# A block kernel on one core: the gemm steps of a recurrence's scan stand behind two of its three small products

## What is computed

```
h = rms_norm(x, pre_norm_gain); proj = h @ w_in
# per head (8 heads of 64), for each of the 1024 rows t:
sa    = state @ a_t
state = state * decay_t + outer(sa, b_t) + outer(v_t, k_t)
y_t   = state @ r_t
# gates: sigmoid(g_attn) * y_attn + sigmoid(g_rwkv) * y_rwkv, z_rwkv in silu
```

## Time and profile before

| | us |
|---|---|
| runs, median of 3 | 2829.97 |
| runs, lowest and highest | 2827.18, 2830.27 |
| profiled execution, its own time | 2842.01 |
| its span, first to last instruction | 2840.2 |
| PE busy in it | 2707.1 (95%) |
| DVE, ACT, POOL busy | 1264.2, 810.1, 1040.2 |
| scan of pair 0, from its first L780 to its last L780 | 785.25 to 842.11 |
| scan of pair 3, likewise | 1288.87 to 1346.89 |

### The profile page before, as it was taken

How to read it: one execution, slowest core, us unless ns; L and a number is a source line. 1 busy time by engine, 2 the same in 40 slices (tenths; PEclk the granted TensorE clock), 3 DMA queues, 4 the chain that set the end, 5 groups by cost and what they waited for, 6 DMA issues and landing times.

```text
span 2840.2 us, 44277 instructions
## 1 busy us (share of the span) xinstructions
PE 2707.1 (95%) x17968; PEld 2176.6 (77%) x17968; DVE 1264.2 (45%) x2338; ACT 810.1 (29%) x1607; POOL 1040.2 (37%) x1318
## 2 busy tenths in 40 slices
PE   6999999997999999999898999999998998999999
PEld 5787777875867777686787888788887887777777
DVE  4225252435847466484531433533335003377743
ACT  3444444444113131220212211211113003255531
POOL 2223232232322231321455133344444456435442
PEclk9999999998999999999998899999999996999999
DMA  3111111111101010111331211111111121111122
GB/s 125 41 45 41 42 45 49 45 45 38 35 17 55 28 49 28 34 46 61 152 119 61 74 45 46 43 45 45 45 45 38 52 67 56 45 38 45 43 109 84
DMA packets 200907, 154.02 MB, mean 54 GB/s; under 512 B 5120, under 2 KB 183680, under 8 KB 200064
## 3 DMA queue, kind: packets, MB, share of 16 engines
q1 hardware_dynamic: 186256, 106.44, 12.6%
q10 hardware_dynamic: 14448, 44.74, 4.1%
HBM read 128.10 MB, written 23.07 MB: 53 GB/s over the span
## 4 chain that ended last, share of the span: by engine, by line
PE 79%; DVE 12%; ACT 6%; issue 1%; POOL 1%; DMA 1%; ACTq 0%; DVEq 0%; SPq 0%; POOLq 0%
PE gemm L527 21%; PE gemm L529 19%; PE gemm L528 19%; ACT prob L1942 3%; DVE neg_logits L1488 2%; DVE prob L1503 2%; PE scores L578 1%; PE scores L769 1%; PE weighted L829 1%; PE weighted L605 1%; PE probs_t L766 1%; PE probs_t L590 1%; PE scores L904 1%; PE scores L758 1%; DVE stats L1492 1%
## 5 line engine op out<-in xcount | busy, mean ns | idle before, releaser
L490 POOL CAST w_hi<-w_raw 128x512 fp32r<-128x512 f32 x360 | 249.1, 692 | 1686.8 <-PE gemm L529 1640.6
L527 PE MATMUL gemm<-h_hi,w_hi 128*128 128x512 f32 x1936 | 799.6, 413 | 9.7 <-ACT q_t L1702 7.6
L529 PE MATMUL gemm<-h_hi,w_lo 128*128 128x512 f32 x1936 | 761.9, 394 | 0.0
L528 PE MATMUL gemm<-h_lo,w_hi 128*128 128x512 f32 x1936 | 761.0, 393 | 0.0
L492 POOL TENSOR_TENSOR w_lo<-w_raw,w_hi 128x256 fp32r<-128x256 f32 x720 | 608.2, 845 | 56.9
L527 PEld LDWEIGHTS gemm<-h_hi,w_hi 128*128 128x128 f32 x1936 | 366.8, 189 | 102.8 <-issue 23.1
L529 PEld LDWEIGHTS gemm<-h_hi,w_lo 128*128 128x128 f32 x1936 | 366.8, 189 | 80.5
L528 PEld LDWEIGHTS gemm<-h_lo,w_hi 128*128 128x128 f32 x1936 | 367.6, 190 | 66.8 <-issue 1.9
L1382 DVE TENSOR_TENSOR scaled_product<-gemm,norm_rstd 128x512 f32<-128x512 f32 x116 | 80.2, 691 | 352.9 <-PE gemm L529 346.8
L527 PE MATMUL gemm<-xn_hi,w_hi 128*128 128x512 f32 x320 | 132.4, 414 | 7.2 <-POOL xn_lo L501 3.7
L1106 DVE CUSTOM_DVE_ANT_0 neg_logits<-scores,bias_tile 128x128 f32<-128x128 f32 (+1 forms) x192 | 67.6, 352 | 148.7 <-PE scores L578 142.9
(11 more groups left out here) (423 smaller groups left out, 4262.9 us busy)
## 6 DMA issues: line engine op xcount, KB each, us to landing
w_raw<-in_w_in SPq DMA_DIRECT2D x73, 512.0 KB, 3.9
w_raw<-in_a_w_in SPq DMA_DIRECT2D x48, 512.0 KB, 3.7
gates_scratch<-o_f ACTq DMA_DIRECT2D x32, 256.0 KB, 2.0
merge_gates<-gates_scratch ACTq DMA_DIRECT2D x4, 2048.0 KB, 15.1
w_raw<-in_a_w_out SPq DMA_DIRECT2D x16, 512.0 KB, 3.4
w_raw<-in_b_w_in SPq DMA_DIRECT2D x16, 512.0 KB, 3.7
x_rows<-in_x SPq DMA_DIRECT2D x8, 512.0 KB, 8.3
w_raw<-in_w_out SPq DMA_DIRECT2D x8, 512.0 KB, 3.4
```

What stands on the lines that cost most here:

```text
L490: Q(pool.tensor_copy(hi[:, ks, :], raw[:, s, ks, :]))
L527: pe.matmul(G[b][:], whi[:, s, k, :], hi(k, h), start=first, stop=False)
L528: pe.matmul(G[b][:], whi[:, s, k, :], lo(k, h), start=False, stop=False)
L529: m = pe.matmul(G[b][:], wlo[:, s, k, :], hi(k, h), start=False, stop=last)
```

## The change

The steps of the scan are no longer dealt to 48 places but to 32: the places `scan{3c}` get none, and the places behind the second and third small product take them all, the earlier chunks first.

```
-            first = sorted(range(3 * NCH), key=lambda i: (i % 3 == 0, i))
-            counts.update({f"scan{i}": rest // len(first) + (first.index(i) < rest % len(first)) for i in range(3 * NCH)})
+            later = [i for i in range(3 * NCH) if i % 3]
+            counts.update({f"scan{i}": rest // len(later) + (later.index(i) < rest % len(later)) if i % 3 else 0 for i in range(3 * NCH)})
```

## The result

| | us |
|---|---|
| before, median of 4 runs | 2830.05 |
| after, median of 4 runs (lowest, highest) | 2847.24 (2845.70, 2849.01) |
| ratio, 95% interval | 1.0053, 1.0032 to 1.0074 |
| profiled execution of after, its span | 2844.6 |

The change makes the kernel slower by 17.2 us, 0.6%. The forecast was 2843.8 us (+13.8), its range 2838.5 to 2851.

What follows compares the result with a forecast made beforehand. PE was taken to bound the kernel, with 79% of the chain and nearly all of the scans. The terms, -25.8 + 41.4 - 2.1 + 0.3 = +13.8 us, on the median of 2829.97 gave 2843.8 us, range 2838.5 to 2851.

Steps and rivals of the forecast that it cites:

- price per moved step: In the scans, each step moved from before L785 to behind it costs 0.26 us; +15.6 us for 60 steps.
- slower still: Rival, 10%: clock dips in chunk 0 of each pair or 0.64 us at each POOL burst; 2846 to 2850 us.
- 1, slots A: From L780 to L785, each of 60 emptied slots shrinks from 1.16 to 0.73 us; -25.8 us.
- 2, steps in slots B and C: From L785 to L792 or L792 to the next L780, each added step costs 0.69 us; +41.4 us for 60.
- 3, stalls of the scalar engine: Waits of L792 for L1797 behind emptying of full halves: 2.16 us goes, 0.10 us comes; -2.1 us.
- 4, vector engine beside POOL: L1309 slowed beside POOL delays L792: one 0.64 us hit against 0.3 us before; +0.3 us, between -0.3 and +2.
- 5, clock in chunk 0: Granted clock in chunk 0: 0, -1.5 us if the one dip goes, +4.4 if the other three pairs dip too.
- The faster rival: Rival, 2%: added steps between L785 and the next L780 hide in the hand-overs, costing nothing; -28 us, 2802 us.
- the one with cheap second steps: Rival, 5%: an added step in the scans costs 0.37 to 0.55 us; time about the same, 2824 to 2836 us.

Runs made afterwards that it cites:

- half the change: Against the kernel before, only chunks 8 to 15 have the slot from L780 to L785 emptied, 28 steps moved instead of 60: 2839.2 us, 1.0021.
- the repeat: The changed kernel, unchanged, run a second time beside the kernel before on the same chip: 2848.5 us, 1.0055.

## Why the prediction was right, and where it was short

Direction and range held, and so did the mechanism of the price per moved step. Its part on the clock did not. The prediction named as a sign of being wrong a granted clock below 1.00 in the scans for more than one chunk: three chunks have it, in both profiles of after. And the rival "slower still", to which it gave 10%, has a cause that is seen here (dips in chunk 0) and a range, 2846 to 2850 us, that holds the measured 2847.24 as the forecast's range does. So the measured time lies where both reach; what happened is the forecast's price per step, and 3.1 of the 4.4 us that a dip in every pair was to cost. Term by term, in the profile, from the first L780 to the last L785 so that all 60 emptied slots count:

| term | forecast | measured |
|---|---|---|
| 1, slots A | -25.8 | -25.8: all 64 slots 0.72 or 0.73 |
| 2, steps in slots B and C | +41.4 | +41.4: 1.85 and 2.13 for two, 2.54 and 2.81 for three, 0.68 to 0.69 each |
| 3, stalls of the scalar engine | -2.2 + 0.1 | -2.2, and 0.39 new where 0.1 was forecast |
| 4, vector engine beside POOL | -0.3 + 0.64 | -0.3 + 0.32 |
| 5, clock in chunk 0 | 0 (-1.5 to +4.4) | +3.1 |
| sum | +13.8 | +16.9 by the rows, +17.1 measured |

Terms 1 and 2 are as they were read: the four empty slots and the doubled ones that the kernel before had were enough to price them. The 0.2 us that the rows leave is rounding, 60 times over.

Terms 3 and 4 were right in their sum and not in their parts, so there the two misses happen to cancel. The stalls that should go went. (In pair 3 most halves now end in slot B and not in slot C as written; the state copy stands ahead of their emptying there too, and nothing shows.) The one at pair 0, chunk 8 was to be 0.10 us and is 0.39: the two copies of the scalar engine begin 0.48 us after the slot A does (822.21 after 821.73), not 0.18 as in the earlier trace rows or 0.19 as in the 15 other halves of r, k and v in after's scans. The rows don't say what holds them; the same 1.55 us stands in four other layouts with this half at this place. In the chunk behind, L1309 took 1.20 us beside POOL, not 1.50. Nor were the 1.50 us "once" before: two more of 1.53 us stand in pairs 1 and 2, under doubled slots B. The two places:

```profile
822.21 0.69 ACT L1659 ACTIVATE v_padded<-gemm,stats 128x512 f32<-128x512 f32 x1 [2.42 <-PE gemm L529]
...
823.65 0.22 ACT L1797 ACTIVATE state_and_v<-max_rows 64x64 f32<-64x64 f32 x1
824.01 0.34 PE L792 MATMUL probs_t<-state_and_v,bk_rows 128*64 128x64 f32 x4 [0.32 <-ACT state_and_v L1797]
...
826.15 1.20 DVE L1309 TENSOR_SCALAR scan_state<-state_and_v,stats 64x64 f32<-64x64 f32 x2
...
827.65 0.34 PE L792 MATMUL probs_t<-state_and_v,bk_rows 128*64 128x64 f32 x4 [0.26 <-DVE state_and_v L1311]
```

Term 5 was mis-sized, and it is most of the miss. "Whether that lowers the clock can be read from the chunks that have them already: 1.00 over 13.4 us" took its evidence from chunks 12 to 15, in the middle of steady work, and carried it to chunk 0, which stands behind an idle PE (1.32 us). The upper bound had the case ("+4.4 if chunk 0 of the other three pairs has one too"); two of the three got it, 1.50 and 1.49 us, and the dip of pair 2 is 0.1 us dearer than before. This +3.1 is read in the profile; of the two kernels without these dips, the one with two steps ahead has runs that fit it; the one with slot A of chunk 0 filled does not. The experiments put a count to it:

| ahead of chunk 0 | its slot A | layouts | dips in chunks 0 |
|---|---|---|---|
| PE idle 1.3 us | filled | 5 layouts, 7 profiles | 3 of 28 |
| PE idle 1.3 us | empty | after, 2 profiles | 6 of 8 |
| two steps | filled or empty | 3 layouts | 0 of 12 |

That both idle stretches have a part is shown by taking away either: the changed kernel loses all its dips with slot A of chunk 0 filled (0 of 8) and with two steps ahead of it (0 of 4). The pair of them is neither always enough (pair 1 of after has both and no dip, twice) nor always needed (3 of 28 with slot A filled). The Trainium skill ("TensorE: Matmul & The Clock Gate", What's actually happening) says that the throttled state is the default and activity releases it. The trace agrees in direction: 6 of 8 with both idle stretches, 0 of 12 with the first one filled. No run here shows why one pair has a dip and its like has none (pair 2 before, pair 1 with half the change).

The step from the span to the median held for a reason that was only half argued. The profiled execution before was 12 us over the median; the prediction said that the extra in the scans does not depend on the run, and in four profiles of the two kernels the scans repeat within 0.1 us. It did not ask where the 12 us were. Against the second profile, 10.2 of them were in two norm stretches at the lower clock, and a comparison of the two spans alone (+4.4 us) would have called the change a quarter of what it is. That the scans' +17.1 us and the medians' +17.2 agree so closely is in part luck: the repeat gave +16.7, and how the clock falls behind the scans moves a single run by more than that.

The faster rival and the one with cheap second steps both needed a second step below 0.46 or 0.55 us; none of the 45 doubled slots B of after is below 1.84 us, 0.68 over a single one. The Trainium skill's 131 ns for a product of 512 columns ("TensorE: Matmul & The Clock Gate", Back-to-back issue gap), by which the change would have gained some 4 us in the prediction's estimate, is not what these products take: 0.23 us from start to start in the doubled slots, and 0.43 in the dips.

## What to carry to other kernels

A piece of work that covers a wait is worth the wait it covers and no more; moved to a place that is covered already, it costs its full length. So price both places from slots that the trace already has, with and without the piece, and look for idle time of the bounding engine before dealing work out: here 0.4% lay in five gaps of 0.5 to 1.3 us a pair. Compare kernels by the stretch that was changed, and check the rest of the span for the clock before believing the difference of two profiles.

## What the runs showed of the hardware

- The granted clock differs between executions of the same kernel in the same stretch: 9 us at 0.50 in one, at 1.00 in the other, worth 7.5 us of 2830 in one norm stretch and up to 4.2 in another. In 58 runs of the kernel before, 2827 to 2847 us, the time goes with the mean granted clock: 0.979 in the shortest, 0.972 in the longest.
- Where PE sat idle for 1.3 us and again for 0.4 us behind the next small product, about 3 us at the lower clock followed in 6 of 8 cases; where it sat idle for the 0.4 us alone, in the other 60 slots A of each execution, no chunk has a dip.
